# The layer norm's second-half sums taken by VectorE instead of TensorE, and three rests per norm handed to GpSimd

## What is computed

```python
def layer_norm(x, g, b):
    mu = jnp.mean(xf, axis=-1, keepdims=True)
    var = jnp.mean(jnp.square(xf - mu), axis=-1, keepdims=True)
    y = (xf - mu) * lax.rsqrt(var + LN_EPS) * g + b
...
x = layer_norm(ALPHA * x + 0.5 * swiglu(x, ffn1_w_gate, ffn1_w_up, ffn1_w_down), ln1_g, ln1_b)
proj = x @ w_in
...
x = layer_norm(ALPHA * x + mixed @ w_o, ln2_g, ln2_b)
x = layer_norm(ALPHA * x + 0.5 * swiglu(x, ffn2_w_gate, ffn2_w_up, ffn2_w_down), ln3_g, ln3_b)
```

## Time and profile before

| | us |
|---|---|
| median of 3 runs | 2511.76 |
| lowest and highest run | 2508.62, 2515.42 |
| the profiled execution, its own time | 2513.35 |
| its span in the trace | 2511.5 |
| TensorE busy in the span | 2488.8 (99%) |
| VectorE, ScalarE, GpSimd busy | 1498.5, 1056.1, 1336.6 |

### The profile page before, as it was taken

One profiled execution on the slowest core, in us unless ns is written; L12 is line 12 of the kernel. 1 busy time (PEld: TensorE's weight loads), 2 busy tenths in 40 slices (PEclk: granted clock), 3 DMA queues, 4 the chain that ended last, 5 costly groups with the idle time before them and its releaser, 6 DMA issues.

```text
span 2511.5 us, 50783 instructions
## 1 busy us (share of the span) xinstructions
PE 2488.8 (99%) x19996; PEld 2373.0 (94%) x19996; DVE 1498.5 (60%) x2640; ACT 1056.1 (42%) x1934; POOL 1336.6 (53%) x840
## 2 busy tenths in 40 slices
PE   9999999999999999999999999999999999999998
PEld 9999999998899999999999999999977788989897
DVE  7556956975453474535575569569754535836366
ACT  3555234235432253636354542342355322537363
POOL 4767435522244456858557674355222444669582
PEclk9999999999999999999999999999999999999999
DMA  5524323432233323333234242234222333334232
GB/s 146 135 67 106 93 77 94 112 81 66 59 81 89 101 76 101 102 101 107 79 90 135 68 114 85 76 94 112 79 68 58 82 99 97 85 101 118 84 102 84
DMA packets 479750, 232.60 MB, mean 93 GB/s; under 512 B 58960, under 2 KB 479056, under 8 KB 479536
## 3 DMA queue, kind: packets, MB, share of 16 engines
q1 hardware_dynamic: 460288, 220.53, 32.9%
q10 hardware_dynamic: 19248, 9.08, 1.5%
HBM read 220.79 MB, written 4.26 MB: 90 GB/s over the span
## 4 chain that ended last, share of the span: by engine, by line
PE 93%; issue 2%; DVE 2%; POOL 1%; ACT 1%; DMA 1%; ACTq 0%; POOLq 0%; SPq 0%; DVEq 0%
PE ps L760 54%; PE ps L928 24%; PE ps L907 4%; PE ps L785 4%; PE ps L1252 1%; PE ps L1291 1%; POOL w_lo L680 1%; PE ps L833 1%; PE ps L1256 1%; PE ps L1267 1%; PE ps L1174 0%; PE ps L1164 0%; PE ps L1269 0%; PE ps L1101 0%; PE ps L1073 0%
## 5 line engine op out<-in xcount | busy, mean ns | idle before, releaser
L680 POOL TENSOR_TENSOR w_lo<-w_raw,w_hi 128x1024 fp32r<-128x1024 f32 (+3 forms) x348 | 732.1, 2113 | 891.4 <-ACT w_hi L1423 891.0
L1423 ACT ACTIVATE w_hi<-w_raw 128x1024 fp32r<-128x1024 f32 (+3 forms) x348 | 315.6, 911 | 548.1 <-PE ps L760 227.3
L760 PE MATMUL ps<-x_hi,w_hi 128*128 128x264 f32 (+2 forms) x1904 | 288.9, 301 | 0.2
L760 PE MATMUL ps<-x_hi,w_lo 128*128 128x264 f32 (+2 forms) x1904 | 280.0, 296 | 0.6 <-POOL w_lo L680 0.6
L760 PE MATMUL ps<-x_lo,w_hi 128*128 128x264 f32 (+2 forms) x1904 | 280.3, 296 | 0.0
L760 PEld LDWEIGHTS ps<-x_hi,w_hi 128*128 128x128 f32 x1904 | 252.2, 188 | 13.5 <-ACT w_hi L1423 0.6
L680 POOL TENSOR_TENSOR w_lo<-w_pair,w_hi 128x512 fp32r<-128x512 f32 x186 | 246.6, 1340 | 30.9 <-ACT w_hi L1423 30.9
L760 PEld LDWEIGHTS ps<-x_hi,w_lo 128*128 128x128 f32 x1904 | 252.4, 188 | 10.3 <-POOL w_lo L680 1.3
L760 PEld LDWEIGHTS ps<-x_lo,w_hi 128*128 128x128 f32 x1904 | 252.5, 188 | 9.0
L680 POOL TENSOR_TENSOR w_lo<-w_sum,w_hi 128x512 fp32r<-128x512 f32 x155 | 202.6, 1320 | 93.5 <-ACT w_hi L1423 92.0
L760 PE MATMUL ps<-hid_hi,w_hi 128*128 128x264 f32 (+1 forms) x1040 | 161.9, 300 | 0.0
(11 more groups left out here) (349 smaller groups left out, 4912.2 us busy)
## 6 DMA issues: line engine op xcount, KB each, us to landing
w_raw<-in_w_in SPq DMA_DIRECT2D x82, 512.0 KB, 3.9
w_pair<-in_ffn_w_gate SPq DMA_DIRECT2D x64, 512.0 KB, 5.2
w_raw<-in_ffn_w_down SPq DMA_DIRECT2D x64, 512.0 KB, 4.1
w_pair<-in_ffn_w_up SPq DMA_DIRECT2D x60, 512.0 KB, 5.3
w_raw<-in_ffn_w_up SPq DMA_DIRECT2D x28, 512.0 KB, 3.9
w_raw<-in_ffn_w_gate SPq DMA_DIRECT2D x24, 512.0 KB, 3.8
w_raw<-in_ffn_w_down SPq DMA_DIRECT2D x32, 384.0 KB, 3.5
w_raw<-in_w_o SPq DMA_DIRECT2D x16, 512.0 KB, 4.0
```

The lines of the kernel that those rows point to most:

```text
L680: pool.tensor_tensor(held(w_lo, c), src, held(w_hi, c).bitcast(f32), ALU.subtract).then_inc(w_split, 1)
L760: ins = nc.tensor.matmul(dst, wk, x[:, k0 + k, tokens], start=first and k == 0 and n == 0, stop=last and k == n_tiles - 1 and n == 2)
L1423: return nc.scalar.activation(out, in_, f, **kw)
```

## The change

There are four parts, all of them in the norm. (1) VectorE now also adds the second half's tiles 5 and 6, and their squares, to the running totals, and TensorE's `second_sums` takes only the totals of tiles 0 to 6 (in front of feature tile 3) and, as `last_sums`, tile 7 (in front of feature tile 5). (2) For feature tiles 5, 6 and 7 of the first half (norms 0 to 4), `scaled` goes to `z` and no longer to PSUM; ScalarE adds the bias in place, then copies to `xh`; GpSimd subtracts the rest from `z`, in front of the second root. (3) In norms 0 and 3 TensorE runs four matmuls of ones by ones (`keep_busy`, 128 columns, added to columns of PSUM that nobody reads) in front of the second output. (4) The counters and one scratch row of the squares follow.

```diff
-SUMS_AT = 4
+SUMS_AT = (3, 5)
+BY_POOL = (5, 6, 7)
+FILLER = 4
...
         def restored(l, which):
-            return (2 * l + which - 1) * KD
+            return l * (2 * KD + len(BY_POOL)) + (0, len(BY_POOL), len(BY_POOL) + KD)[which]
...
                 for n in range(SLOTS - 1):
                     split(l, c0 + n)
+                n = l * 3 + which
+                cols = norm_span(n).halves[0]
+                for k in BY_POOL:
+                    pool.wait_ge(ln_hi, n * 2 * KD + (k + 1))
+                    pool.wait_ge(x_ready[0], (n + 1) * KD + k)
+                    pool.tensor_tensor(xl[:, k, cols], z[:, k, cols], xhf[:, k, cols], ALU.subtract).then_inc(x_ready[0], 1)
                 root(l, which, 1)
                 split(l, c0 + SLOTS - 1)
...
+            def keep_busy(n):
+                for _ in range(n):
+                    nc.tensor.matmul(ps[:, 0, 384:384 + P], ones[:], ones[:], start=False, stop=True, skip_group_check=True)
...
-                         between={(0, 0): lambda: second_sums(n, 4, 5), (0, 1): lambda: second_sums(n, 6),
-                                  (SUMS_AT, 0): lambda: second_sums(n, 7)} if n >= 0 else {})
+                         between={(0, 1): lambda: keep_busy(0 if n % 3 else FILLER), (SUMS_AT[0], 0): lambda: second_sums(n),
+                                  (SUMS_AT[1], 0): lambda: last_sums(n)} if n >= 0 else {})
...
+            def second_sums(n):
+                pe.wait_ge(ln_sums, n * 3 + 4)
+                for src, bank in ((stat[:, 1], 5), (stat[:, 2], 7)):
+                    token_sums(n, 1, src, bank, True, False)
+
+            def last_sums(n):
+                k = KD - 1
+                pe.wait_ge(z_half[1], n * 4 + (k + 1))
+                token_sums(n, 1, z[:, k], 5, False, True).then_inc(ln_stat, 1)
+                pe.wait_ge(ln_square, n * 12 + (k + 5))
+                token_sums(n, 1, stat[:, 3 + k % 2], 7, False, True).then_inc(ln_stat, 1)
...
-                if h == 0:
+                if h == 0 and k not in BY_POOL:
                     ACTV(xh[:, k, sp.halves[0]], ps[:, 1 + 2 * (k % 2), 0:sp.half], ACT.Identity,
                          bias=par[:, col:col + 1]).then_inc(ln_hi, 1)
                     return
-                ACTV(z[:, k, sp.halves[1]], z[:, k, sp.halves[1]], ACT.Identity, bias=par[:, col:col + 1]).then_inc(ln_out[1], 1)
+                ACTV(z[:, k, sp.halves[h]], z[:, k, sp.halves[h]], ACT.Identity, bias=par[:, col:col + 1]).then_inc(ln_out[h], 1)
...
-                    if h and k > WHOLE:
+                    if h and k == KD - 1:
                         return
...
-                    scaled = lambda k: z[:, k, cols] if h else ps[:, 1 + 2 * (k % 2), 0:sp.half]
+                    scaled = lambda k: z[:, k, cols] if h or (k in BY_POOL and n < 3 * DEPTH - 1) else ps[:, 1 + 2 * (k % 2), 0:sp.half]
...
-                            if h == 0 and k >= 2:
+                            if h == 0 and k >= 2 and not (k in BY_POOL and n < 3 * DEPTH - 1):
...
-                            add_half_square(WHOLE, 1, 9).then_inc(ln_sums, 1)
+                            st.done(add_half_square(WHOLE, 1, 9))
...
-                        if k and h == 0 and n < 3 * DEPTH - 1:
+                        if k and h == 0 and n < 3 * DEPTH - 1 and k - 1 not in BY_POOL:
...
                         if h == 0 and k in TAKES_IN[nk]:
+                            if TAKES_IN[nk][k] == 6:
+                                st.done(add_half_square(5, 1, 10))
                             take_half(TAKES_IN[nk][k], 1)
+                            if TAKES_IN[nk][k] == 7:
+                                add_half_square(6, 1, 11).then_inc(ln_sums, 1)
```

More of the change, by code:

```diff
@@ L697, in norm @@
                     split(l, c0 + n)
+                n = l * 3 + which
[4 more added lines that the diff above has]
+                    pool.tensor_tensor(xl[:, k, cols], z[:, k, cols], xhf[:, k, cols], ALU.subtract).then_inc(x_ready[0], 1)
                 root(l, which, 1)
                 split(l, c0 + SLOTS - 1)
-                cols = norm_span(l * 3 + which).halves[1]
+                cols = norm_span(n).halves[1]
                 for k in range(KD):
@@ L1414, in _ @@
                 ffn(l, 1)
-            second_sums(3 * DEPTH - 1, *range(WHOLE, KD))
+            second_sums(3 * DEPTH - 1)
+            last_sums(3 * DEPTH - 1)
             spread_mean(3 * DEPTH - 1, 1)
@@ L1488, in norm_tile @@
                     return
-                ACTV(z[:, k, sp.halves[1]], z[:, k, sp.halves[1]], ACT.Identity, bias=par[:, col:col + 1]).then_inc(ln_out[1], 1)
+                ACTV(z[:, k, sp.halves[h]], z[:, k, sp.halves[h]], ACT.Identity, bias=par[:, col:col + 1]).then_inc(ln_out[h], 1)
                 if n == 3 * DEPTH - 1:
                     return
-                act.wait_ge(ln_out[1], n * KD + (k + 1))
-                ACTV(xh[:, k, sp.halves[1]], z[:, k, sp.halves[1]]).then_inc(ln_hi, 1)
+                if h == 0:
+                    act.wait_ge(ln_out[0], restored(l, which) + (k + 1 if which else k - BY_POOL[0] + 1))
+                else:
+                    act.wait_ge(ln_out[1], n * KD + (k + 1))
+                ACTV(xh[:, k, sp.halves[h]], z[:, k, sp.halves[h]]).then_inc(ln_hi, 1)
             def norm_out(l, which, k):
@@ L1518, in layer_norm @@
                 for k in range(KD):
+                    if k == BY_POOL[0]:
+                        norm_out(l, which, k - 1)
                     norm_tile(l, which, k, 0)
-                    if k:
+                    if k and (k < BY_POOL[0] or l * 3 + which == 3 * DEPTH - 1) and k != BY_POOL[0]:
                         norm_out(l, which, k - 1)
@@ L1525, in layer_norm @@
                         round_ahead(l, bd + 6 + rounded_in.index(k))
-                norm_out(l, which, KD - 1)
+                if l * 3 + which == 3 * DEPTH - 1:
+                    norm_out(l, which, KD - 1)
                 for k in range(KD):
@@ L2599, in _ @@
                 st.close()
-DVE_STEPS = 396
+DVE_STEPS = 408
 _WEIGHTS = ("ffn1_w_gate", "ffn1_w_up", "ffn1_w_down", "w_in", "mla_w_uq", "mla_w_ukv", "mla_w_o", "conv_w_out",
```

10 lines of the change are left out of this document (4 added, 6 removed).

## The result

| | us |
|---|---|
| before, median of 8 runs | 2511.36 (2508.3 to 2517.68) |
| changed, median of 8 runs | 2524.04 (2518.55 to 2527.24) |
| changed / before | 1.0048, 95% interval 1.0034 to 1.0062 |
| changed, the span of the profiled execution | 2525.0 (2511.5 before) |

The changed kernel is slower by 0.5%. That is rival B; the time lies inside the stated range, but not where the likeliest case had it: the range was wide enough to hold rival B too. The profiled execution of the changed kernel was the second longest of its eight (2527.23).

A forecast was written before the change was run, and what follows sets the result against it. TensorE was taken as the bound, 93% of the chain. Five stretches at 54.55 against 54.68 us, with norm 5, gave +0.3: 2513.65; one clock fall of 3.0 made 2516.6 us, range 2506 to 2527.

The forecast's parts named there:

- rival B: TensorE's waits behind takes 6 and 7 drop the clock in two or three middle norms, 3 to 4 us each; 0.38.
- the likeliest case: None or one clock fall in all, 2513.65 to 2518.3 us, down to 2511 if GpSimd is quick; chance 0.48.
- The bound, and the path: TensorE holds 93% of the chain; time counts from second-half first sums to `spread_mean`, five stretches, 54.68 us together.
- The middle norms at full clock: Norms 1, 2 and 4: TensorE waits 1.0 and 1.6 us for takes 6 and 7; stretch 10.5, +0.8 in norm 1.
- Norms 0 and 3: Filler 0.8 us, waits for take 6, tile 2's rest and tile 7 (1.35); stretch 11.55 us.
- Why their clock stays: Norms 0 and 3: filler in front and sums split by matmuls keep full clock; 6.1 us of low pieces gone.
- The forecast's other figure: Cost of the change in the profiled execution, had before run without its low clock pieces: 6.4 us.
- The clock in the middle norms: Norms 1, 2 and 4: a fall costs 1.5 to 4.6 us; one counted at 3.0, giving 2516.6.
- Norm 5: The totals wait for one VectorE addition behind take 7 before TensorE's sums: 0.45 us (0 to 0.9).
- The sum: Five stretches at full clock 54.55 against 54.68 us; with norm 5 +0.3, so 2513.65 for the profiled execution.
- Rivals C and D: C: takes over when TensorE comes, 2500 us, 0.10. D: norms 0 and 3 still fall, 2519.8 us, 0.04.
- rival C: VectorE keeps up and tile 7 is no wait, so each norm keeps its saving: 13.5 us less, 2500; 0.10.

The follow-up runs named there:

- the best form: The changed kernel with six filler matmuls in norms 1, 2 and 4 and none in norms 0 and 3: 2513.5 us, ratio 1.0005.

## Why the prediction came out as it did

*The bound, and the path.* Right. Each stretch was paid by TensorE.

*The middle norms at full clock.* Right: 10.5 was forecast, 10.44 measured. The waits were forecast at 1.0 and 1.6 and were 0.79 and 1.55, the second output 3.75 behind TensorE's arrival and was 3.68.

*Norms 0 and 3.* Right in the sum, 11.55 against 11.56, with errors that cancel. The wait for tile 2's rest was 0.68 instead of 1, tile 7's 1.17 instead of 1.35. GpSimd's rest took 0.74, 1.5 times VectorE's 0.49. The Trainium skill, "GPSIMD Engine Reference", section "4.1 Engine selection", has about two, so the trace is below the page. I missed 0.25 in `last_tiles`, where TensorE now waits for a take that VectorE's addition holds up.

*Why their clock stays.* The step failed. I put it down to filler in front and to the spread of the sums. Without filler they stayed as well, and in the second trace of before they ran at full clock with the old sums. What is left: in no trace did norm 0 or 3 fall with only twenty-four sum instructions in it (sixteen stretches with the change's sums, two with tiles 5 and 6 left out), and with forty-eight three of ten did. I had also set the absence of falls here against 6.1 of falls in before, as if these came in every run. The forecast's other figure, 6.4 more with no fall on either side, is the one that the runs bear out, at about 5 for the best form and 7.5 for the changed kernel (5.9 + 1.1 + 0.5).

*The clock in the middle norms.* This step was mis-sized. I counted one fall at 3.0; the trace has three, of 13.54 − 10.44 = 3.1, 1.5 and 5.4 us, 10.0 together, and the next has two, of 5.6 and 4.2. Each of the two traces has one more, of 3.4 us of low clock, outside the norms. So B was the case, at the price that it gave (3.8 each in the mean, 3.3 measured). It got less than the forecast because both falls in the one trace that I had came behind sums without a wait. I read from that that waits are harmless. The Trainium skill's rule in "TensorE: Matmul & The Clock Gate", section "A second HAM failure mode: psum-queue depth-cycling", had the right sign; eight falls in nine stretches agree with it. It says nothing of falls without idle, of which the kernel before has two in each trace.

*Norm 5.* 0.45 forecast, 0.52 measured, and that was the cheap case. In four of the six traces with the wait of 2.03 the clock was low before the second `spread_mean`, and norm 5 took 24.6 to 25.1 from its first one to the end, 1.6 to 2.1 more than before's 23.0. I had not thought of the clock there. It is not the wait alone: two of the eight traces without it had a low clock there too, at 23.9 and 24.3.

*The sum.* Without the falls (10.0) and the 2.1 outside the norms the changed span would be 2525.0 − 12.1 = 2512.9, 1.4 over before's with its falls in it, where I had 0.3: the two waits in `last_tiles`, 0.3 each, and some 0.1 in each middle norm. Rivals C and D did not occur.

*Against rival C.* The saved sums were never worth 8.8. The run without them shows what they were: 0.37 in norm 1, the one middle norm at full clock there, as a wait stood behind them.

## What to carry to other kernels

Work on the bounding engine that stands in front of a wait is nearly free, and taking it away buys only the distance to the wait: here 1.78 us of sums bought 0.37. Find the semaphore that comes next, and the time at which it is given, before counting a saving. And an idle moment of 1.5 us on TensorE may cost more than 1.5: in eight places of nine the clock fell around it, for 1.5 to 5.6 us more. Where the idle can't be avoided, matmuls that nobody reads, put into it, gave 8 of 13 us back. A low clock in one trace is one draw; take a second trace before building on where it stood, and put the granted clock of every run beside its time: here two kernels whose medians can't be told apart differ by 5 us where neither loses its clock.

## What the runs showed of the hardware

The clock of one and the same kernel falls in different places from run to run: in the kernel before twice in each trace, in norms 0 and 3 once and in 1 and 2 the other time, each with 1.5 or 4.6 us. The spread of its runs goes with it: of 23 on one chip, the shortest (2506.6) had a mean granted clock of 0.997 and the longest (2521.2) one of 0.992.

The 2.1 us outside the norms are a wait that the profile calls "issue", in the last matmuls of the state part between norms 0 and 1, and a fall behind it. The wait was 1.96 in the changed kernel and 1.41 before, which leaves 1.5, what the short falls in the norms cost (second row: a stretch, with its clock at 0.50):

```profile
520.89 0.35 PE L1180 MATMUL ps<-s_state,s_out 64*64 64x66 f32 x8 [1.96 <-issue]
522.40:525.70 3.30, 3.30 (x18) 0.50 0.58 163
```

In the second traces the wait was 0.18 (before) and 1.11 (changed), with no fall there. It changes from run to run of one kernel, so I don't lay it to the change. Nor does a wait there always bring a fall: with filler in 1, 2 and 4 only it was 1.69, at full clock.
